# A third score tile in the stick-breaking stage, with its mask and the memory's scaling on VectorE

## The reference

```python
z = jnp.einsum('bhtd,bhsd->bhts', q_blk, kh) * scale
before = (key_pos[None, :] < q_pos[:, None])[None, None]
log_beta = jax.nn.log_sigmoid(z)
log_one_minus = jnp.where(before, jax.nn.log_sigmoid(-z), 0.0)
between = lax.cumsum(log_one_minus, axis=3, reverse=True) - log_one_minus
weights = jnp.exp(jnp.where(before, log_beta + between, -jnp.inf))
o = jnp.einsum('bhts,bhsd->bhtd', weights, vh)
...
k, v = jnp.split(rmsnorm(mem, mem_kv_norm) @ w_kv, 2, axis=-1)
```

## Time and profile before

| | us |
|---|---|
| median of 3 runs | 2538.96 |
| the runs | 2538.47, 2545.68, 2538.96 |
| the profiled execution | 2545.0 |
| its span, first to last instruction | 2542.8 |
| busy: PE, DVE, ACT, POOL | 2452.1, 1236.4, 891.8, 105.8 |
| stick-breaking stage, first score to first `mix_out` matmul | 1818.99 to 1997.27 |
| start of score(1) | 1828.18 |
| one unit from issue to landing | 4.8 |

### The profile page before, as it was taken

One profiled execution on the slowest core, in us unless ns is written; L12 is line 12 of the kernel. 1 busy time (PEld: TensorE's weight loads), 2 busy tenths in 40 slices (PEclk: granted clock), 3 DMA queues, 4 the chain that ended last, 5 costly groups with the idle time before them and its releaser, 6 DMA issues.

```text
span 2542.8 us, 30263 instructions
## 1 busy us (share of the span) xinstructions
PE 2452.1 (96%) x12270; PEld 2041.2 (80%) x12270; DVE 1236.4 (49%) x1436; ACT 891.8 (35%) x1202; POOL 105.8 (4%) x115
## 2 busy tenths in 40 slices
PE   7989999999999999999999999999888999999998
PEld 6658888888898788888788888798767777888886
DVE  6677543366746533332444431556664544444423
ACT  3353333213344433331333321344433444333311
POOL 0210000000102000000000000000120000000000
PEclk9999999998999999999999999999987999999999
DMA  8125522473232122222222222221111222222221
GB/s 347 57 91 217 196 92 99 149 286 110 102 94 82 67 99 99 99 99 95 76 96 97 99 99 99 95 84 67 51 49 38 81 72 78 99 88 94 99 99 66
DMA packets 40405, 267.34 MB, mean 105 GB/s; under 512 B 4378, under 2 KB 5658, under 8 KB 9218
## 3 DMA queue, kind: packets, MB, share of 16 engines
q1 hardware_dynamic: 31248, 219.87, 24.2%
q0 software_dynamic: 5696, 40.37, 4.1%
q10 hardware_dynamic: 3378, 5.91, 0.8%
HBM read 263.90 MB, written 2.24 MB: 105 GB/s over the span
## 4 chain that ended last, share of the span: by engine, by line
PE 85%; DVE 9%; ACT 4%; issue 1%; DMA 0%; POOL 0%; POOLq 0%; DVEq 0%; SPq 0%; ACTq 0%
PE bank L227 25%; PE bank L228 25%; PE bank L229 25%; DVE w_lo L214 1%; ACT w_hi L210 1%; PE bank L2138 1%; DVE work L457 1%; PE bank L2200 1%; PE bank L2212 1%; PE bank L1864 1%; PE bank L330 1%; DVE work L441 1%; DVE work L2278 1%; PE bank L1860 1%; DVE h_lo L467 1%
## 5 line engine op out<-in xcount | busy, mean ns | idle before, releaser
L227 PE MATMUL bank<-h_hi,w_hi 128*128 128x512 f32 x1800 | 710.5, 395 | 5.7 <-DVE w_lo L214 2.5
L228 PE MATMUL bank<-h_lo,w_hi 128*128 128x512 f32 x1800 | 702.5, 390 | 0.0
L229 PE MATMUL bank<-h_hi,w_lo 128*128 128x512 f32 x1800 | 702.3, 390 | 0.0
L214 DVE TENSOR_TENSOR w_lo<-raw,w_hi 128x2048 fp32r<-128x2048 f32 x192 | 440.1, 2292 | 477.7 <-ACT w_hi L210 477.7
L210 ACT ACTIVATE w_hi<-raw 128x2048 fp32r<-128x2048 f32 x192 | 366.2, 1908 | 412.7 <-PE bank L229 409.2
L227 PEld LDWEIGHTS bank<-h_hi,w_hi 128*128 128x128 f32 x1800 | 339.1, 188 | 83.2 <-issue 6.7
L229 PEld LDWEIGHTS bank<-h_hi,w_lo 128*128 128x128 f32 x1800 | 339.1, 188 | 71.4
L228 PEld LDWEIGHTS bank<-h_lo,w_hi 128*128 128x128 f32 x1800 | 339.2, 188 | 70.0 <-issue 1.4
L229 PE MATMUL bank<-g_hi,w_lo 128*128 (+1 forms) x704 | 273.9, 389 | 0.0
L227 PE MATMUL bank<-g_hi,w_hi 128*128 (+1 forms) x704 | 273.9, 389 | 0.0
L228 PE MATMUL bank<-g_lo,w_hi 128*128 (+1 forms) x704 | 273.9, 389 | 0.0
(11 more groups left out here) (314 smaller groups left out, 2869.1 us busy)
## 6 DMA issues: line engine op xcount, KB each, us to landing
raw<-stream SPq DMA_DIRECT2D x192, 1024.0 KB, 4.8
work<-stream POOLq DMA_DIRECT2D x19, 1024.0 KB, 6.9
h_plain<-stream POOLq DMA_DIRECT2D x16, 1024.0 KB, 5.4
work<-stream SPq DMA_DIRECT2D x13, 1024.0 KB, 12.3
work<-mlstm_rows ACTq DMA_DIRECT2D x8, 512.0 KB, 4.8
x<-xT SPq DMA_DIRECT2D x1, 2048.0 KB, 9.8
outT<-work SPq DMA_DIRECT2D x8, 256.0 KB, 2.3
work<-mlstm_rows ACTq DMA_DIRECT2D x8, 192.0 KB
```

What stands on the lines that cost most here:

```text
L214: nc.vector.tensor_tensor(w_lo[:, slot(m), :], raw[:, slot(m), :], w_hi[:, slot(m), :], ALU.subtract).then_inc(lo_split, 1)
L227: nc.tensor.matmul(out, stationary[0], moving[0], start=first, stop=False)
L228: nc.tensor.matmul(out, stationary[0], moving[1], start=False, stop=False)
L229: return nc.tensor.matmul(out, stationary[1], moving[0], start=False, stop=last)
```

## The change

Three things. z gets a third tile in `h_plain`, free in this stage, and the copy of z(h) waits for the weighted sum of head h-3. The mask of the weights moves from POOL to VectorE, behind the four subtractions of its head. The memory is scaled by gain and root in one step on VectorE in iteration 1, eight instructions of 128x256 ahead of l(1), in place of two on POOL; the root is taken in iteration 0. Further, the three `gate_rows` of iteration 0 move behind everything of iteration 1; ScalarE takes the exp of the weights ahead of the split of the unit, and evacuates the last unit ahead of the last head's exp.

```diff
-            z = [area(2048, 1280), area(18432, 1280)]
+            z = [area(2048, 1280), area(18432, 1280), h_plain[:, 3, 512:1792]]
...
                         dve.wait_ge(self.s_z, h + 1)
-                        if h >= 2:
-                            dve.wait_ge(self.s_o, h - 1)
+                        if h >= 3:
+                            dve.wait_ge(self.s_o, h - 2)
...
+                    if i == 1:
+                        mem.scale(dve)
...
+                        dve.wait_ge(self.s_x, TB * h + TB)
+                        for a in range(TB):
+                            z = self.z[h % 3][:, self.diag(a)]
+                            ins = nc.vector.tensor_tensor(z, z, table("neg_strict"), ALU.add)
...
-                    if i == 0:
-                        for b in range(3):
+                    if i == 1:
+                        mem.low(dve)
+                        split_next_lo(dve, mem.m_kv - 1)
+                        for b in range(4):
                             hg.tail.gate_rows(dve, b)
-                    if i == 1:
-                        hg.tail.gate_rows(dve, 3)
-                        split_next_lo(dve, mem.m_kv - 1)
-                        mem.low(dve)
...
-                    if 3 <= i <= self.H:
+                    if 3 <= i <= self.H + 1:
                         mem.evacuate(act, i - 3)
-                        split_next_hi(act, mem.m_kv + i - 3)
...
+                    if 3 <= i <= self.H:
+                        split_next_hi(act, mem.m_kv + i - 3)
...
                     if i == 0:
+                        mem.take_root(act, st)
+                        split_next_hi(act, mem.m_kv - 1)
+                    if i == 1:
+                        mem.high(act)
                         hg.tail.group_squares(act, st, hg.H - 1)
                         hg.tail.take_roots(act, st, 0, hg.H)
-                        split_next_hi(act, mem.m_kv - 1)
-                    if i == 1:
-                        mem.root_and_high(act, st)
                     if i == self.H + 1:
-                        mem.evacuate(act, 6)
...
+            def scale(self, dve):
+                dve.wait_ge(self.s_root, 1)
+                for k in range(KC):
+                    c = slice(k * N_MEM, k * N_MEM + N_MEM)
+                    nc.vector.scalar_tensor_tensor(self.t[:, c], self.mt[:, c], col("mem_kv_norm", k), self.rstd,
+                                                   ALU.mult, ALU.mult).then_inc(self.s_scaled, 1)
```

More of the change, by code:

```diff
@@ L2207, in sum_values @@
                     pe.wait_ge(self.s_out, h)
-                w = self.z[h % 2]
+                w = self.z[h % 3]
                 for t in range(TB):
@@ L2270, in vector @@
                     if h < self.H:
-                        z, e, l = self.z[h % 2], self.e[h % 2], self.l[h % 2]
+                        z, e, l = self.z[h % 3], self.e[h % 2], self.l[h % 2]
                         dve.wait_ge(self.s_z, h + 1)
-                        if h >= 2:
-                            dve.wait_ge(self.s_o, h - 1)
+                        if h >= 3:
+                            dve.wait_ge(self.s_o, h - 2)
                         for a in range(TB):
@@ L2295, in vector @@
                             dve.wait_ge(self.s_suf, n + 1)
-                            z = self.z[h % 2][:, self.seg(a)]
+                            z = self.z[h % 3][:, self.seg(a)]
                             nc.vector.scalar_tensor_tensor(z, bank[:, 4 + n % 2, a * P:S], -1.0, z, ALU.mult,
                                                            ALU.add).then_inc(self.s_x, 1)
-                    if i == 0:
-                        for b in range(3):
+                        dve.wait_ge(self.s_x, TB * h + TB)
+                        for a in range(TB):
+                            z = self.z[h % 3][:, self.diag(a)]
+                            ins = nc.vector.tensor_tensor(z, z, table("neg_strict"), ALU.add)
+                            if a < TB - 1:
+                                st.add(ins)
+                            else:
+                                ins.then_inc(self.s_nx, 1)
+                    if i == 1:
+                        mem.low(dve)
+                        split_next_lo(dve, mem.m_kv - 1)
+                        for b in range(4):
                             hg.tail.gate_rows(dve, b)
-                    if i == 1:
-                        hg.tail.gate_rows(dve, 3)
-                        split_next_lo(dve, mem.m_kv - 1)
-                        mem.low(dve)
                     if 2 <= i < 4:
@@ L2335, in scalar @@
                         act.wait_ge(self.s_nx, h + 1)
-                        nc.scalar.activation(self.z[h % 2], self.z[h % 2], ACT.Exp).then_inc(self.s_a, 1)
+                        nc.scalar.activation(self.z[h % 3], self.z[h % 3], ACT.Exp).then_inc(self.s_a, 1)
+                    if 3 <= i <= self.H:
+                        split_next_hi(act, mem.m_kv + i - 3)
                     h = i
@@ L2367, in scalar @@
                 split_next_hi(act, mem.m_kv + 6)
[L2369 to L2376, removed]
         class Mix:
@@ L2462, in sum_squares, with take_root @@
                 last.then_inc(self.s_ms, 1)
-            def root_and_high(self, act, st):
+            def take_root(self, act, st):
                 act.wait_ge(self.s_ms, 1)
@@ L2467, in root_and_high, with high @@
                 nc.scalar.activation(self.rstd, self.logs, ACT.Exp, scale=-0.5).then_inc(self.s_root, 1)
-                act.wait_ge(self.s_scaled, 2)
+            def high(self, act):
+                act.wait_ge(self.s_scaled, KC)
                 nc.scalar.activation(mem_hi.rearrange("p a n -> p (a n)"), self.t, ACT.Copy).then_inc(self.s_hi, 1)
@@ L2798, in _ @@
             memory.gpsimd(pool)
-            mix.sb.gpsimd(pool)
         @block.scalar
```

## The result

| | before | after |
|---|---|---|
| median, us | 2540.19 (4 runs) | 2510.85 (4 runs) |
| runs | 2538.47 to 2545.68 | 2506.66 to 2513.56 |
| profiled execution, span | 2545.0, 2542.8 | 2508.91, 2506.1 |
| first score to first `mix_out` matmul | 178.3 | 137.1 |

The ratio is 0.9879, 95% interval 0.9857 to 0.9902. The time is 29.3 us less by the medians, 36.1 by the two profiled executions; 35.0 and 39.5 were forecast. The absolute 2504 was 6.9 us low.

What follows compares the result with a forecast made beforehand. It took a ring of TensorE and VectorE, closed by the release of two z tiles, to bound the stage. Start 11.9, loop 25.4, end 2.6, less 0.45, made 39.5 us off 2545.0: 2505.5, stated as 2504, range 2496 to 2519.

Steps and rivals of the forecast that it cites:

- The ring and its release: Loop turns 3 to 7: with a third z tile the 2.67 us waits go; a turn is TensorE's 15.09 us.
- The start: Iterations 0 to 2: suffix sum 2 of iteration 2 may start at 1859.1 instead of 1870.99, gain 11.9 us.
- The end: Iterations 8 and 9: a 1.20 us wait and 1.4 of half clock go, gain 2.6; last head loses 0.45.
- The sum: Whole stage: 11.9 + 25.4 + 2.6 - 0.45 = 39.5 us gained.
- the 12.1 us of clock in the loop: Part of the loop's 25.4 us gain: without waits the clock stays full, so 12.1 us of half clock go.
- The 13.35 us of waits: Part of the loop's 25.4 us gain: TensorE's waits over five turns go.
- this stage holds most of the half clock, so I say 2504: Absolute time, chosen between 2505.5 and 2499.5 by where the 6 us between profiled execution and median lie.
- The low end of the range: Total of 2496 us, if the whole 6 us lie elsewhere and the scale is at its low end.
- Rival 1: Loop: the clock goes on falling, waits go but 12.1 + 1.4 of clock stay; time 2518, chance 0.11.
- Rivals 2 to 4: TensorE waits in another form, 2522, 0.08; half clock through stage, at worst 2605, 0.02; third tile frees nothing, 2530, 0.02.

Runs made afterwards that it cites:

- e1: The kernel before with only the third z tile added, mask on POOL and ScalarE's order as before: 2522.13 us, ratio 0.9908.
- e4: The changed kernel with two z tiles again, all else as changed: 2538.12 us, ratio 0.9971 against the kernel before.
- e5: The kernel before, unchanged, timed and profiled a second time: 2544.37 us, ratio 1.0011.
- e6: The changed kernel, unchanged, timed and profiled a second time: 2509.22 us, ratio 0.986 against the kernel before.
- e7: The kernel before with six unused TensorE matmuls in the wait before suffix sum 2 of turns 2 to 7: 2537.57 us, ratio 0.9982.
- e2: The kernel before with only the mask of the weights moved to VectorE, two z tiles: 2541.27 us, ratio 0.9986.
- e8: The changed kernel with twelve unused matmuls in iteration 1's stop, gates and hg's scaling one iteration later, last evacuation behind last exp: 2502.01 us, ratio 0.9829.
- e3: The kernel before with only the start changed (root in iteration 0, memory scaled on VectorE in iteration 1, gates behind): 2536.39 us, ratio 0.9978.

## Why the prediction was right, and where its size was off

**The ring and its release: right.** The chain arrives ahead of TensorE, no wait takes the place of the 2.67, and a turn is TensorE's own work: 14.83 instead of the 15.09 taken. The 0.26 had stood in TensorE's busy time on both sides of the wait: suffix sums 2 and 3 take 1.14 behind a wait and 1.04 without one, and from suffix sum 0 to the wait it is 5.04 before, 4.89 now. I read it as the drain and refill of the pipeline; that is not shown. e1 shows the tile alone does it, e4 that nothing else does.

**The start: right within 0.1.** Suffix sum 2 of iteration 2 came 12.0 us earlier against the first score (11.9). Inside it the eight scalings took 3.25 (2.7 taken) and the stop 5.75 (5); the agreement of the whole to 0.1 is closer than its parts were, and partly luck. VectorE's copy of z(2) began 31.1 us behind the first score, as forecast, and its chain set the time. TensorE, which the forecast had arriving together with it, was there 0.93 earlier: its half clock in the start lasted about 10 us (a granted clock of 0.87 over 40.0), not the 12.1 taken. The price of a scaling also had a slip: by length between 0.225 and 1.49 a 128x256 comes to 0.37 and eight to 2.9, not to 0.34 and 2.7.

**The end: right.** 2.9 gained to the last piece (2.6 taken), wait 1.84 (1.95 taken). What was missed is that the clock can fall behind this wait, about 3 us when it does. That is no price of the new order alone: behind the old waits of 1.20 and 1.49 it fell too, in one of the five profiles that have them (e1).

**The sum: right for the profiled pair.** 12.0 + 26.6 + 2.9 - 0.4 = 41.1 us of the stage, 39.5 forecast.

**The term mis-sized for the medians is the 12.1 us of clock in the loop.** It came from one execution in which three of five turns had half clock; e5, the same program, had 1.5 in one turn. The 13.35 us of waits were in both. Counting the kernel's half clock from one profile made the gain too large by up to that difference, and the stage of that execution (178.3) was 10.7 us over that of e5. The clocks of all runs say the same. The span of a run times what its mean granted clock lacks to 1.00 is an estimate of what half clock cost it. It averages 56 us in the 61 runs of the kernel before that were timed beside the experiments and 42 in the eight of the changed kernel, so by this estimate clock gives about 13 us of the gain; in the first profiled pair it is 18 (58.5 and 40.1).

The reading behind the term was also off. The prediction says that by the rows a 2.67 wait was followed by full clock twice and by a fall three times. But the first turn of the earlier trace rows starts behind a wait of 0.29 only:

```profile
1870.99 1.14 PE L2223 MATMUL bank<-work,tab 128*128 128x256 f32 x6 [0.29 <-DVE work L2297]
```

The last stretch starts behind a wait of 2.67 and has 0.92. So full clock followed once, and a fall four times. In the five profiles with this wait the clock of the stretch behind it is below 1.00 in 18 of 26 cases, from two of five (e5) to five of six (e4).

**A second step that was off** is "this stage holds most of the half clock, so I say 2504". The stage's clock was 0.83 in the first profile, which is about 30 of the 58.5 us, and 0.90 in e5, 17 of 53: half of the half clock, and a third. In the eleven other profiles the first score, behind unchanged work, starts at 1819.1 to 1826.2; the first profile's 1818.99 is the lowest of the twelve. Its total of 2545.0 was an early start and a heavy stage. Putting the middle start (1823.0) with a stage of 137.1 and 546 behind it gives a span of 2506 and with the 2 to 3 us around it 2508 to 2509, near the 2509.2 of e6. The low end of the range has a slip as well: 2499.5 less the 0.9 of the cheaper scale is 2498.6, not 2496.

Rival 1 (the clock still falls in the loop) is refuted as far as the profiles go: none of the 30 loop turns of the six three-tile profiles shows it. Rivals 2 to 4 are out by the turns of 14.83. The spread ahead of the stage is clock as well: up to the first score TensorE is busy for 1767.5 us in e7 and for 1774.7 in e5, with the same work, and the first score comes 7.1 us later. What stays open is behind which idle times the clock falls there, and how often; twelve profiles are too few for a frequency.

## What to carry to other kernels

In a ring of two engines look at which tile release closes it; one more tile can turn a chain of waits into the busy time of one engine, and moving work between engines around it (e2) did nothing by itself in the loop. Check a new order for its last iteration too: here the evacuation ahead of the last exp took back what the faster mask had won, and e8, which leaves it behind that exp, has no wait there. And never read the cost of half clock from one profile: take the waits as certain, the clock as a draw, and profile the kernel before a second time.

## What the runs showed of the hardware

- The same wait of 2.67 us was followed by a fall of the clock or not in the same program: the turns behind it were 17.75 to 17.77 without one, and 19.1 to 19.3, 22.5 or 23.8 with one, in five profiles of four kernels (before twice, e2, e3, e4). The Trainium skill, "TensorE: Matmul & The Clock Gate", section "A second HAM failure mode: psum-queue depth-cycling", says that frequent short idles make the clock oscillate; the traces agree for idles of 2.67 us, show single falls behind idles of 1.84 (two of five), 1.49 and 1.20 (one of five each), and none in a turn that has only hand-overs.
- Keeping TensorE busy with unused matmuls held the clock at 1.00 in every turn (e7), with turns of 17.66 to 17.77 us, as long as the full-clock turns of e5 with their waits.
- VectorE's operation on two tensors and a scalar took 0.41 a piece at 128x256 (eight in 3.25, L2453), above the 0.37 by length.
